# Group 0's weights in three more places, an earlier split of the output weights, and a shorter router, in a one-core transformer kernel

## The reference, cut to what matters

```python
mod = silu(c) @ ada_w + ada_b                      # six vectors: SH1, SC1, G1, SH2, SC2, G2
h = rms_norm(x, norm_g[0]) * (1 + sc1) + sh1
x = x + g1 * (stick_breaking_attention(q, k, v of h @ sb_w_in) @ sb_w_out)      # 16 heads of 64
h = rms_norm(x, norm_g[1]) * (1 + sc2) + sh2
grp = argmax(h @ w_grp + b_grp)                    # 4 groups
p_grp = softmax(group logits)[grp]
in_grp = (h @ w_exp + b_exp)[the 8 experts of grp] # 32 experts in all
p_in, top_i = top_k(softmax(in_grp), 2)
gate = p_grp * p_in / sum(p_in)
y[token] = sum over its 2 experts of gate * ((silu(h @ w_gate[e]) * (h @ w_up[e])) @ w_down[e])
x = x + g2 * y
```

## Time and profile before

| | us |
|---|---|
| median of 3 runs | 1350.35 |
| profiled execution | 1357.34 |
| its span, first to last instruction | 1355.6 |
| TensorE (PE) busy | 1112.6 (82%) |
| VectorE (DVE) busy | 507.8 (37%) |
| ScalarE (ACT) busy | 399.2 (29%) |
| GpSimd (POOL) busy | 41.1 (3%) |

### The profile page before, as it was taken

One profiled execution on the slowest core, in us unless ns is written; L12 is line 12 of the kernel. 1 busy time (PEld: TensorE's weight loads), 2 busy tenths in 40 slices (PEclk: granted clock), 3 DMA queues, 4 the chain that ended last, 5 costly groups with the idle time before them and its releaser, 6 DMA issues.

```text
span 1355.6 us, 16510 instructions
## 1 busy us (share of the span) xinstructions
PE 1112.6 (82%) x7014; PEld 824.7 (61%) x7014; DVE 507.8 (37%) x597; ACT 399.2 (29%) x463; POOL 41.1 (3%) x69
## 2 busy tenths in 40 slices
PE   5999997565666667566559999979999998999997
PEld 2895575131331213132229999869987876999985
DVE  4344523011010101011035555455754695555543
ACT  2335523000000000000134444344544543444432
POOL 1001300000000000000000000000000120000000
PEclk8899897888888779788878999989999999899999
DMA  9977552999999999999976555454454354555430
GB/s 371 316 282 253 187 244 76 423 397 422 423 422 422 419 402 422 422 422 422 421 277 219 186 187 184 155 196 150 162 180 177 124 186 140 167 182 182 182 127 31
DMA packets 119778, 357.92 MB, mean 264 GB/s; under 512 B 9492, under 2 KB 55208, under 8 KB 95144
## 3 DMA queue, kind: packets, MB, share of 16 engines
q1 hardware_dynamic: 117512, 351.54, 67.5%
q10 hardware_dynamic: 2208, 5.54, 1.2%
HBM read 356.01 MB, written 1.05 MB: 263 GB/s over the span
## 4 chain that ended last, share of the span: by engine, by line
PE 64%; DMA 24%; DVE 5%; ACT 2%; SPq 2%; issue 2%; POOL 0%; DVEq 0%; ACTq 0%
PE psum L1787 16%; PE psum L1788 16%; PE psum L1789 16%; DMA ring<-in_moe_w_down_dram 14%; DMA ring<-in_moe_w_gate_dram 8%; PE psum L2015 4%; PE psum L2030 3%; PE psum L1994 1%; DMA ring<-in_ada_w_dram 1%; PE psum L1829 1%; SPq L651 1%; PE psum L2039 1%; PE psum L1898 1%; ACT hn L796 1%; SPq L628 1%
## 5 line engine op out<-in xcount | busy, mean ns | idle before, releaser
L1445 DVE TENSOR_TENSOR wl<-ring,wh 128x2048 fp32r<-128x2048 f32 x102 | 234.3, 2302 | 246.5 <-ACT wh L970 246.3
L970 ACT ACTIVATE wh<-ring 128x2048 fp32r<-128x2048 f32 x102 | 195.2, 1916 | 310.6 <-PE psum L1789 310.1
L1787 PE MATMUL psum<-hTh,wh 128*128 128x256 f32 x832 | 237.5, 285 | 4.6 <-DVE hTl L1464 2.9
L1788 PE MATMUL psum<-hTl,wh 128*128 128x256 f32 x832 | 237.0, 285 | 0.0
L1789 PE MATMUL psum<-hTh,wl 128*128 128x256 f32 x832 | 236.7, 284 | 0.0
L2015 PE MATMUL psum<-ring,m_xT 128*32 128x512 f32 x1024 | 138.2, 696 | 72.7 <-DMA ring<-in_moe_w_up_dram 48.6
L1787 PEld LDWEIGHTS psum<-hTh,wh 128*128 128x128 f32 x832 | 161.0, 194 | 5.3 <-issue 5.2
L1788 PEld LDWEIGHTS psum<-hTl,wh 128*128 128x128 f32 x832 | 160.9, 193 | 0.0
L1789 PEld LDWEIGHTS psum<-hTh,wl 128*128 128x128 f32 x832 | 160.9, 193 | 0.0
L2015 PEld LDWEIGHTS psum<-ring,m_xT 128*32 128x32 f32 x1024 | 40.7, 125 | 164.4 <-issue 164.4
L2030 PE MATMUL psum<-ring,m_hT 128*32 128x512 f32 x512 | 85.4, 827 | 57.9 <-DMA ring<-in_moe_w_down_dram 57.9
(11 more groups left out here) (320 smaller groups left out, 1413.1 us busy)
## 6 DMA issues: line engine op xcount, KB each, us to landing
ring<-in_moe_w_gate_dram SPq DMA_DIRECT2D x64, 1024.0 KB, 18.9
ring<-in_moe_w_up_dram SPq DMA_DIRECT2D x64, 1024.0 KB, 12.6
ring<-in_moe_w_down_dram SPq DMA_DIRECT2D x64, 1024.0 KB, 18.6
ring<-in_ffn_w_in_dram SPq DMA_DIRECT2D x44, 1024.0 KB, 7.5
ring<-in_w_mix_in_dram SPq DMA_DIRECT2D x32, 1024.0 KB, 6.1
ring<-in_ada_w_dram SPq DMA_DIRECT2D x24, 1024.0 KB, 9.3
ring<-in_ffn_w_out_dram SPq DMA_DIRECT2D x20, 1024.0 KB, 6.1
ring<-in_sb_w_in_dram SPq DMA_DIRECT2D x12, 1024.0 KB, 15.3
```

Of the source, the lines that this page charges most:

```text
L970: a.activation(dst, src, ACT.Copy).then_inc(split_h, 1)
L1445: v.tensor_tensor(split_half(h, wl), raw_half(h), split_half(h, wh).bitcast(FP32), ALU.subtract)\
L1787: t.matmul(dst, sh, mh, start=first, stop=False, skip_group_check=True)
L1788: t.matmul(dst, sh, ml, start=False, stop=False, skip_group_check=True)
```

## The change

It has six parts.

1. **Places.** Step 0 no longer puts units 6, 7 and 8 into ring slots: they go to three 2 MB areas outside the ring (`spare`). SP's order for step 0 becomes 0, 1, 2, 6, 3, 4, 5, 7, 8, 9, 10, 11, each with a wait of its own; step 1 is written out in the order 1, 0, 2, 3, ..., 11; the loop starts at 2. TensorE's step 0 is written out of its loop.
2. **Splits.** Halves 12 and 13 are split in p = 4 and p = 5; 13 and 15 share a buffer, whose high part moves to the area of `x`. Half 15 so waits for the product of half 13.
3. **G2.** The two units of `ada(G2)` are used in p = 7 and p = 8 instead of both in p = 8.
4. **Bias.** The 16-record product in p = 7 becomes a multiply and a reduce on VectorE and one matmul, after the first output product; the column spread goes there too.
5. **Routing.** Experts are chosen from masked logits, not from softmax values; only the difference of the two top logits goes through exp. The subtraction of 1 from `posm` falls away (the index `iota` starts at 1).
6. **Gather.** TensorE's gather of a step waits for `m_sel`, no longer for `m_wsel`.

```diff
-early_at = [(REST + 14336, REST + 14336 + HALF), (REST + 4096, REST + 4096 + HALF), (REST + 10240, REST + 2048)]
+early_at = [(REST + 14336, REST + 14336 + HALF), (REST + 4096, REST + 4096 + HALF), (x_at, REST + 2048)]
...
+FIRST_ORDER = (0, 1, 2, 6, 3, 4, 5, 7, 8, 9, 10, 11)
+spare = [area(f"spare{i}", REST + at, SLOT) for i, at in enumerate((4096, 0, 16304))]
+def first_place(u):
+    if 6 <= u < 9:
+        return spare[u - 6], spare_in[u - 6], 32
+    n = NA + u if u < RING_A else NA + RING_A + {9: 0, 10: 2, 11: 3}[u]
+    return slot_a(n), wa_in[n % RING_A], 32 * (n // RING_A + 1)
...
-    return h % 2 if h < EARLY_QKV else (1, 2, 0, 1)[h - EARLY_QKV]
+    return h % 2 if h < EARLY_QKV else (1, 2, 0, 2)[h - EARLY_QKV]
...
-expert_units(NA, 0, 0, main, wa_in)
-with sp.Fori(1, NEG) as g:
+for u in FIRST_ORDER:
+    dst, landed, _ = first_place(u)
+    if u < RING_A:
+        await_unit_used(sp, units_a[NA - RING_A + u])
+    elif u == 6:
+        await_full(sp, ("out", 0, 0))
+    elif u == 7:
+        await_full(sp, ("out", 1, 1))
+    elif u == 8:
+        await_full(sp, ("logits",))
+    else:
+        sp.wait_ge(main.used, {9: 1, 10: 3, 11: 4}[u])
+    expert_unit(u, 0, dst, landed)
+for u in (1, 0, 2, 3, 4, 5, 6, 7, 8, 9, 10, 11):
+    sp.wait_ge(main.used, {1: 2, 0: 10, 2: 11, 3: 12, 4: 5, 5: 6}.get(u, UNITS_PER_GROUP + u + 1 - RING_A))
+    expert_unit(u, 1, slot_a(NA + u), wa_in[(NA + u) % RING_A])
+with sp.Fori(2, NEG) as g:
...  (early_high)
-    if h == EARLY_QKV:
+    if h == EARLY_QKV or h == EARLY_QKV + 1:
         await_early_used(act, EARLY_QKV - 1)
-    elif h == EARLY_QKV + 1:
-        await_full(act, ("z", HEADS - 1))
     elif h == EARLY_QKV + 3:
-        await_early_used(act, EARLY_QKV)
+        await_early_used(act, EARLY_QKV + 1)
...  (ScalarE's and VectorE's attention loops, early_high and early_rest)
-if p == PAIRS - 2:
-    early_high(12)
-if p == PAIRS:
-    early_high(13)
+if p in (4, 5):
+    early_high(EARLY_QKV + p - 4)
...  (router_columns on VectorE, called after early_rest(14) and not in p == 7)
+link(v.tensor_tensor(shift_w, wr, acol[:, SH2, :].unsqueeze(2).to_broadcast([P, KD, 36]), ALU.mult))
+v.tensor_reduce(shift_p, shift_w.rearrange("p k n -> p n k"), AX, ALU.add).then_inc(bias_s, 1)
...  (after the two sums into x of output product 0, 0; early_rest(15) moves behind those of 0, 1)
+router_bias()
...  (VectorE, routing)
 dve.wait_ge(consts, 11)
-first_max(ohg, gl, gmax, GROUPS, t4)
+link(v.tensor_reduce(gmax, gl, AX, ALU.max))
 v.tensor_tensor(gl_e, gl, wide(gmax, GROUPS), ALU.subtract).then_inc(r_diff, 1)
-link(v.tensor_scalar(t4, ohg, -1.0, None, ALU.add))
-link(v.tensor_scalar(negm, t4, 1e30, None, ALU.mult))
-link(v.tensor_tensor(by_group(t32), by_group(el), wide8(negm), ALU.add))
-link(v.tensor_reduce(emax, t32, AX, ALU.max))
-v.tensor_tensor(ex, t32, wide(emax, EXPERTS), ALU.subtract).then_inc(r_diff, 1)
-dve.wait_ge(r_exp, 1)
-link(v.tensor_reduce(gsum, gl_e, AX, ALU.add))
-dve.wait_ge(r_exp, 2)
-link(v.tensor_reduce(esum, ex, AX, ALU.add))
-link(v.reciprocal(esum, esum))
-link(v.tensor_tensor(one_of, ex, wide(esum, EXPERTS), ALU.mult))
-link(v.tensor_tensor(by_group(pm), by_group(one_of), wide8(t4), ALU.add))
-first_max(oh1, pm, p1, EXPERTS, t32)
-link(v.scalar_tensor_tensor(pm, oh1, -4.0, pm, ALU.mult, ALU.add))
-first_max(oh2, pm, p2, EXPERTS, t32)
+first_max(t4, gl, gmax, GROUPS, t4, ALU.not_equal)
+link(v.scalar_tensor_tensor(by_group(masked), wide8(t4), -1e30, by_group(el), ALU.mult, ALU.add))
+link(v.tensor_reduce(top1, masked, AX, ALU.max))
+first_max(oh1, masked, top1, EXPERTS, t32)
+link(v.scalar_tensor_tensor(pm, oh1, -2e30, masked, ALU.mult, ALU.add))
+link(v.tensor_reduce(top2, pm, AX, ALU.max))
+v.tensor_tensor(e2, top2, top1, ALU.subtract).then_inc(r_diff, 1)
+first_max(oh2, pm, top2, EXPERTS, t32)
 v.tensor_tensor(chosen, oh1, oh2, ALU.add).then_inc(r_sel, 1)
...  (first_max without its first reduce; the gates' sum and quotients after chosen)
-link(v.tensor_scalar(posm, posm, -1.0, None, ALU.add))
...  (TensorE, after output product 0, 0)
+pe.wait_ge(bias_s, 1)
+b = open_bank(pe, ("bias",))
+filled(t.matmul(b[:, 0:36], ones, shift_p, start=True, stop=True), ("bias",))
+pe.wait_ge(spread_s, 2)
+b = open_bank(pe, ("perm",))
+for i in range(2):
+    last = t.matmul(b[:, KD * i:KD * i + KD], spread[:, i, :], em8, start=True, stop=True)
...  (expert_group)
-    pe.wait_ge(S.sel, it + 1)
+    pe.wait_ge(S.steps, steps)
     ... gather matmuls
+    pe.wait_ge(S.sel, it + 1)
-with pe.Fori(0, NEG) as g:
-    expert_group(g, main, NA, wa_in)
+expert_group(0, main, NA, wa_in, 1)
+with pe.Fori(1, NEG) as g:
+    expert_group(g, main, NA, wa_in, g + 1)
```

More of the change, by code:

```diff
@@ L373, in build_program @@
         wa_in = [sem(f"wa{s}_in") for s in range(RING_A)]
+        spare_in = [sem(f"spare{s}_in") for s in range(3)]
         wb_in = [sem(f"wb{s}_in") for s in range(RING_B)]
@@ L911, in _ @@
             act.wait_ge(r_diff, 2)
-            a.activation(route[:, 64:128], route[:, 64:128], ACT.Exp).then_inc(r_exp, 1)
+            a.activation(route[:, 64:66], route[:, 64:66], ACT.Exp).then_inc(r_exp, 1)
             act.wait_ge(rs2_s, 1)
@@ L1284, in _ @@
             early_rest(14)
+            router_columns()
             for u in range(2):
@@ L1296, in _ @@
                     if u == 0 and i == 0:
+                        router_bias()
+                    if u == 0 and i == 1:
                         early_rest(15)
@@ L1916, in _ @@
                     ada(ADA_ORDER[2 + p // 2], p % 2)
-                if p == PAIRS:
-                    ada(G2, 0)
-                    ada(G2, 1)
+                if p >= PAIRS - 1 and p <= PAIRS:
+                    ada(G2, p - PAIRS + 1)
                 if p - 1 in ADA_AT:
                     ada_col(ADA_ORDER.index(ADA_AT[p - 1]))
-                if p == PAIRS - 1:
-                    pe.wait_ge(rt_s, 64)
-                    pe.wait_ge(cols_s, 5)
-                    b = open_bank(pe, ("bias",))
-                    for k in range(KD):
-                        last = t.matmul(b[:, 0:36], acol[:, SH2, k:k + 1].to_broadcast([P, P]), wr[:, k, :],
-                                        start=(k == 0), stop=(k == KD - 1))
-                    filled(last, ("bias",))
-                    b = open_bank(pe, ("perm",))
-                    pe.wait_ge(spread_s, 2)
-                    for i in range(2):
-                        last = t.matmul(b[:, KD * i:KD * i + KD], spread[:, i, :], em8, start=True, stop=True)
-                    filled(last, ("perm",))
             for p in range(KD):
@@ L1986, in _, with expert_group @@
                 await_copied(pe, name)
-            def expert_group(it, S, first, landed):
+            def expert_group(it, S, first, landed, steps):
                 pe.wait_ge(S.acc, it + 1)
-                pe.wait_ge(S.sel, it + 1)
+                pe.wait_ge(S.steps, steps)
                 for c in range(KD):
@@ L2004, in two_slots @@
                     both = []
-                    for n in (first + u, first + u + 1):
-                        pe.wait_ge(landed[n % RING_A], it * 64 + 32 * (n // RING_A + 1))
-                        both.append(slot_a(n).rearrange("p (e k n) -> p e k n", e=2, k=rows))
+                    for v in (u, u + 1):
+                        if S is main and isinstance(it, int):
+                            flat, s, count = first_place(v)
+                        else:
+                            flat, s, count = later_place(first, v, it, S, landed)
+                        pe.wait_ge(s, count)
+                        both.append(flat.rearrange("p (e k n) -> p e k n", e=2, k=rows))
                     return both
```

87 lines of the change are left out of this document (43 added, 44 removed).

## The result

The changed kernel took **1332.64 us** (median of 4 runs, 1330.72 to 1333.98), the kernel before 1350.19 beside it: ratio 0.9868, 95% interval 0.9848 to 0.9887. The forecast was 1331.0. The profiled execution took 1331.31, span 1329.6, mean granted clock 0.925. The two profiled spans differ by 26.0, the medians by 17.6: the first profiled execution of before was 7.0 above its median, which the prediction took off.

The account below looks back on a forecast made before the run. Weight transfers at 422 GB/s were taken to bound the expert stage. Places -14.9, Ts -3.4 (-7.9 + 1.8 + 3.1 + 2.0 = -1.0, router -2.4) and gaps -1.0 give -19.3: 1350.35 - 19.3 = 1331.0 us, range 1325 to 1339.

Parts of the forecast that it names:

- Places, -14.9: Expert stage: transfers of units 6, 7 and 8 land in the earlier DMA hole, taking 3 x 4.97 = 14.9 us out.
- gaps -1.0: DMA gaps at the expert stage's turns: the first turn's 2.1 us gap should go; -1, bounds -4 and +3.
- Rival D: Expert stage: no gain from the places because TensorE can't follow the transfers; 1347 us, chance 0.03.
- rival C: Slower than before: the in-order queue at unit 0 of step 1 lets DMA run dry; chance 0.03.
- Attention, -7.9: First output matmul moves from 171.4 to 163.5: bias product and spread leave, waits shrink, clock stays up; -7.9 us.
- the lower of the two bounds, -2: Attention's smallest gain, -2 us: clock falls as before, 4.9 goes, 1.8 comes and the waits stay.
- Output products, +6.9: Two new TensorE waits in the output products, +1.8 and +3.1 us, and the clock they cost, +2.0.
- half 15's copy: Output products: half 15 waits for product (0,1), table and squares queue behind it, TensorE waits +3.1 us, bounds +2.5 and +4.
- Router, -2.4: Expert choice: fewer operations, none waiting for exp; the gather starts at 215.2 instead of 217.66, -2.4 us, bounds -1.6 and -3.3.
- Gather and first pair, 0: Gather and first expert pair: clock as before, no change, 0 us, bounds -1.5 and +1.5.
- Ts, -3.4: Moment the first expert pair is used and DMA gets going: 3.4 us earlier, at 228.6.
- rival B: Only the places pay: attention's clock falls as before, output-product waits eat the router's gain; -10 to -14, 1338 us, chance 0.17.

Follow-up runs that it names:

- e9: The kernel before with part 1 (the places) and nothing else but three small areas moved: 1333.4 us, ratio 0.9861.
- k1: The kernel before, unchanged, profiled a third time: 1353.86 us, ratio 1.0017.
- e2: The changed kernel with the output weights split where they were before, and unit 6 issued after output product (1,1): 1328.48 us, ratio 0.9837.
- e8: The changed kernel with the old splits, the spread behind product (0,1), and the gather no longer behind the g2b copies: 1324.53 us, ratio 0.9811.
- a0: The changed kernel again, unchanged, in a second measurement: 1332.44 us, ratio 0.9859.
- e7: e6 with the spread behind product (0,1) and the gather no longer behind the g2b copies: 1325.28 us, ratio 0.9808.
- e6: The changed kernel with ScalarE's table load and first two squares ahead of half 15's copy: 1328.76 us, ratio 0.983.
- e3: The changed kernel with parts 3 and 4 undone (bias product and spread on TensorE in attention, both G2 units in p = 8): 1331.2 us, ratio 0.9856.
- k0: The kernel before, unchanged, profiled a second time: 1352.38 us, ratio 1.0008.
- e1: The changed kernel with the three places undone (units 6 to 11 in the ring again), TensorE's first step still written out: 1349.92 us, ratio 0.9978.
- e4: The changed kernel with the old routing (softmax values, 28 operations, the subtraction of 1 from the positions): 1333.15 us, ratio 0.9867.
- e5: The changed kernel with the gather waiting for m_wsel again in every step: 1332.86 us, ratio 0.9859.

## Why the prediction was right, and where it wasn't

The time is in the range and 1.6 above the forecast. One step of the sum, the attention, had its reason wrong, and one term was missing; that the number came so close is in part luck. By its own steps:

- **Places, -14.9, gaps -1.0: right.** D-Ts fell from 452.7 to 454.5 (three profiles) to 437.6 and 438.9: 14 to 17. e9 confirms it by itself: 17.2 in the medians, of which 1.7 is the first pair's. The chain of arguments from Ts on held: no gap in the first turn (422 and 419 GB/s), one smaller gap later. It was nearer than worked out: the last down pair of step 0 begins at Ts + 18.8 and step 1's first pair at Ts + 40.0 (37.8 in the forecast), because unit 11 was put at Ts + 17.7 without a working (its own 1.2 + 3 x 4.97 gives 16.1) and its pair took 5.34 and not 3.6; the pair still ends at about Ts + 43.5, before the Ts + 46.0 to which DMA has work. What would have spoken against it (a window below 400, unit 0 of step 1 behind a dry queue) is not there. Rival D has nothing for it, rival C neither.
- **Attention, -7.9: the number right, the reason half wrong.** This is the step that failed. It read the fall of the clock after the 2.29 us wait in one profile as a property of the kernel and booked its end as a gain. k1 has the wait without the fall, and so do e2, e8 and e9; two of six profiles with this wait fell, both of the kernel before. Against executions of the same kind the part is worth 3.1: the bias product and the spread at full clock are 1.97 + 0.29 + 0.61 and not 4.9. By the segments 2.0 of the 3.1 are parts 3 and 4 (T-A 53.65 in e9, 51.67 in e2) and 1.1 is part 2 (50.54). That lay near the lower of the two bounds, -2, which is itself not the sum of its terms: 4.9 out and 1.8 in are -3.1.
- **Output products, +6.9: right.** 6.4 in the first profile (39.85 - 33.42), 4.9 in a0. The terms: the spread's bank 1.02 of waiting and 0.58 of work (+1.8 forecast; e7 shows 1.3), half 15's copy 3.21 (+3.1), and the clock behind it. e6 takes the last two away and gets 4.8.
- **Router, -2.4: right.** 2.6 against the first profile, 1.9 against k1 and e9. `chosen` ends at 207.2, and, as the step had it, the gather doesn't start when the mask could be made but when ScalarE's g2b copies are done:

```profile
206.98 0.23 DVE L1391 TENSOR_TENSOR route<-route 128x64 f32<-128x64 f32 x1
...
211.22 0.43 DVE L1419 TENSOR_TENSOR m_sel<-iota,posm 128x256 f32<-128x256 f32 x1 [1.81 <-ACT g2b L965]
```

- **Gather and first pair, 0: a missed term.** The first pair is 1.7 shorter in every kernel with the first step written out. The prediction had the pair's clock as before and gave that edit no price. S0-G varies from 7.2 to 9.0 over all profiles and shows no clear difference.
- **Ts, -3.4.** From A it moved by 7.4 against the two profiles with the fall, by 1.7 to 2.2 against k1. The forecast lies between, because the part that was too large stood in one sum with a term that was missing. Here is the luck: with 3.1 in place of 7.9 the sum would have been -14.5 (1335.9), and with the missing 1.7 -16.2 (1334.2), both in the range but further off.

So parts 2 to 6 together, forecast at -3.4, brought nothing that the segments show (Ts-A of the change against e9: +0.3 and -0.2) and 0.8 to 1.0 in the medians, which can't be told from nothing. The gain is that of part 1: 17.2 in e9's median. Of it 1.7 is the first pair's by the segments, which leaves 15 to 16 for the three places; no run has the written-out step alone, so this division isn't shown in a time. In its balance this is rival B ("only the places pay"), but at the forecast's time, since B carried the fall of the clock as a cost of the changed kernel too.

Open: in what share of executions the clock falls in the kernel before (two of three profiles; the timed runs have no trace); what separates e3's two longest runs from the other four; why the written-out step keeps the clock up; and why k1, with Ts 5.0 earlier than k0, has a span only 2.1 shorter: 2.7 of the difference come back behind the last down pair, in code that the change doesn't touch.

## What to carry to other kernels

When a queue of transfers stands still because its ring is full, and memory of a finished stage lies idle, put the next stage's transfers there: the gain is bytes over bandwidth, and it can be read off one window of the profile beforehand. A copy that is moved to a later moment takes all that stands behind it in its engine's queue along; ask for each moved instruction what it waits for now and who needs the one behind it. Before a fall of the clock in one profile is booked as a cost that an edit removes, look at it in a second profile of the same kernel.

## What the runs showed of the hardware that was not expected

- The granted clock behind the same wait of 2.29 us in the same program: 0.50 in k0 (bias product 3.63), 1.00 in k1 (1.97).
- The attention of the other kernels has the same two outcomes: behind a wait of 1.77 the clock fell in e1 (0.52 in 150 to 152) and not in e4, e5 and e6; behind 2.29 it stayed up in e2, e8 and e9; in e7 it fell behind 2.08.
- Clock falls came after shorter waits as well: in e8 the wait before the gather is 1.49, and the gather takes 6.75; in e7, behind the same 1.49, it takes 5.44, and in the changed kernel 5.16 behind a wait of 2.96. The timeline of TensorE and a window of e8 (columns as in the earlier trace rows) show it, the clock at 0.50:

```profile
207.15 6.75 PE L2022 MATMUL psum<-m_sel,hn 128*128 128x128 f32 x32 [1.49 <-DVE m_sel L1429]
```

```profile
207.00:212.00 5.00, 4.85 (x23) 4.88 (x24) 0.43 (x2) 2.02 (x3) 0.00 (x0) 0.50 1.00 405
```

  The length of the wait right before a piece of work doesn't alone tell its clock.
- The stage before A, the same code in all fourteen profiles, ended between 109.2 and 113.2.
